# Two-layer hybrid encoder step: eleven weight places and three buffers of gathered rows in the expert stage

## What is computed

```python
def hier_moe(x, w_rg, b_rg, w_re, b_re, w_eg, w_eu, w_ed):   # 4 groups of 8 experts, hidden width 128
    g_w, g_idx = lax.top_k(pg, 1)                            # one group per row
    e_w, e_idx = lax.top_k(pe, EXP_TOPK)                     # two experts of that group
    ...
    for g in range(N_GROUPS):
        h = jax.nn.silu(jnp.einsum('nd,edf->nef', xf, w_eg[g])) * jnp.einsum('nd,edf->nef', xf, w_eu[g])
        out = out + jnp.einsum('nef,efd->nd', h * gate[:, g, :, None], w_ed[g])
    return out.reshape(b, t, d)

h = h + hier_moe(rms_norm(h, norm2), ...)
y = rms_norm(h, final_norm)                                  # after the last layer
```

## Time and profile before

| | us |
|---|---|
| runs: median (lowest to highest of 3) | 1532.16 (1531.15 to 1532.2) |
| profiled execution | 1534.14 |
| its span, first to last instruction | 1532.4 |
| TensorE busy in it | 1341.7 (88%) |
| VectorE, ScalarE, GpSimd busy | 527.1, 342.6, 220.3 |
| mean granted TensorE clock | 0.943 |
| DMA, mean over the span | 137 GB/s |

### The profile page before, as it was taken

One profiled execution on the slowest core, in us unless ns is written; L12 is line 12 of the kernel. 1 busy time (PEld: TensorE's weight loads), 2 busy tenths in 40 slices (PEclk: granted clock), 3 DMA queues, 4 the chain that ended last, 5 costly groups with the idle time before them and its releaser, 6 DMA issues. The chain is left out here.

```text
span 1532.4 us, 15151 instructions
## 1 busy us (share of the span) xinstructions
PE 1341.7 (88%) x5592; PEld 739.8 (48%) x5592; DVE 527.1 (34%) x1445; ACT 342.6 (22%) x773; POOL 220.3 (14%) x357
## 2 busy tenths in 40 slices
PE   6999899999999993987599999999999999569771
PEld 5654446544444452554385544564444445345440
DVE  1278884111011117221245789621100111442114
ACT  2142566100001010221213326531000010012112
POOL 5011051000000001232140200500000000023213
PEclk9999999999999995999799999999999999879986
DMA  8302102504105025899671220231060140649975
GB/s 227 110 12 56 56 1 68 165 0 137 70 0 206 0 78 195 311 411 402 252 192 59 56 63 1 63 103 68 0 205 0 45 161 0 233 157 410 408 293 216
DMA packets 94795, 210.32 MB, mean 137 GB/s; under 512 B 25392, under 2 KB 34832, under 8 KB 94720
## 3 DMA queue, kind: packets, MB, share of 16 engines
q1 hardware_dynamic: 81792, 183.90, 33.6%
q0 software_dynamic: 12928, 25.43, 4.8%
HBM read 196.29 MB, written 27.78 MB: 146 GB/s over the span
## 5 line engine op out<-in xcount | busy, mean ns | idle before, releaser
L689 PE MATMUL bank<-ring,xt 128*128 128x512 f32 (+1 forms) x1440 | 571.9, 553 | 2.8 <-issue 1.8
L689 PEld LDWEIGHTS bank<-ring,xt 128*128 128x128 f32 x1440 | 273.2, 192 | 272.6 <-issue 258.4
L1592 DVE TENSOR_TENSOR scr<-scr,bank 128x512 f32<-128x512 f32 x20 | 13.8, 688 | 368.6 <-PE bank L960 368.6
L507 POOL TENSOR_SCALAR stat<-stat 128x1 f32<-128x1 f32 (+1 forms) x27 | 10.3, 380 | 799.1 <-ACT uv L1106 617.2
L1250 ACT ACTIVATE scr<-bank,stat 128x512 f32<-128x512 f32 x40 | 25.3, 684 | 347.9 <-PE bank L689 347.8
L1026 PE MATMUL bank<-ring,xt 128*64 128x256 f32 x480 | 70.7, 402 | 17.1 <-issue 17.1
L720 PE MATMUL bank<-ring,xt 128*128 128x512 f32 x160 | 76.8, 614 | 0.0
L1026 PE MATMUL bank<-qkv,xt 128*64 128x256 f32 x256 | 70.2, 436 | 7.2 <-issue 7.2
L960 PE MATMUL bank<-ring,att 128*128 128x512 f32 x160 | 72.5, 596 | 2.2 <-ACT sgt L1242 1.8
L960 PE MATMUL bank<-ring,sgt 128*128 128x512 f32 x160 | 71.9, 592 | 0.0
L689 PE MATMUL bank<-more,xt 128*128 128x512 f32 x160 | 70.3, 592 | 0.0
(11 more groups left out here) (262 smaller groups left out, 1737.6 us busy)
## 6 DMA issues: line engine op xcount, KB each, us to landing
ring<-in_w_in SPq DMA_DIRECT2D x12, 2048.0 KB, 9.2
ring<-in_w_ed SPq DMA_DIRECT2D x36, 512.0 KB, 18.5
ring<-in_w_eg SPq DMA_DIRECT2D x30, 512.0 KB
ring<-in_w_eu SPq DMA_DIRECT2D x30, 512.0 KB
qkv<-in_w_eg SPq DMA_DIRECT2D x16, 512.0 KB
qkv<-in_w_eu SPq DMA_DIRECT2D x16, 512.0 KB
ring<-in_w_out SPq DMA_DIRECT2D x4, 2048.0 KB, 11.9
more<-in_w_ed SPq DMA_DIRECT2D x16, 512.0 KB, 12.6
```

What stands on the lines that cost most here:

```text
L689: mm = pe.matmul(out, xt[:, k, t * P:(t + 1) * P], rhs[:, k, :], start=(k == 0), stop=(k == KD - 1))
L1592: V.tensor_tensor(t1, t1, b[2][:, :], ALU.mult)
```

## The change

The expert stage gets an eleventh weight place and loses one of its four buffers of gathered rows; the space for the place comes from that buffer, from 24 more columns of `uv`, and from a part of `att`. Expert 10 is loaded ahead of the stage, just before the writes of x to `xd`. The loads in the stage go by pairs of units (11, 12), (13, 14) and so on, each after the block that used the place. The one-hots move from `att` to `uv`, the final norm's weights from `att` (loaded by GpSimd early in the last stage) to `qkv` (loaded by SP after block 16), the five targets of the squares become one with a wait between them, and the clearing of the gathered buffers' last columns moves behind the wait for the table.

```diff
-PLACES = 10
-XBUF = 4
+PLACES = 11
+XBUF = 3
-RING_FREE = 3 * PLACES // 2
+RING_FREE = 15
...
-        uv = sb("uv", [P, 2, NT, BLK])
+        uv_flat = sb("uv", [P, 2 * NT * BLK + 24])[:, :]
+        uv = uv_flat[:, 0:2 * NT * BLK].rearrange("p (c t w) -> p c t w", c=2, t=NT)
...
-        fin_gain = att_flat[:, 0:D]
-        onehot = att_flat[:, 0:2 * NT * (BR + UNITS)].rearrange("p (m c) -> p m c", m=2 * NT)
+        onehot = uv_flat[:, XW:XW + 2 * NT * (BR + UNITS)].rearrange("p (m c) -> p m c", m=2 * NT)
+        fin_gain = qkv_flat[:, 2048:2048 + D]
...
-                  (xt_flat[:, 2560:4608], ring_flat[:, 15360:16384])]
+                  (xt_flat[:, 2560:4608], ring_flat[:, 15360:16384]),
+                  (uv_flat[:, XW * XBUF:XW * XBUF + 2048], att_flat[:, 0:D])]
...
-        junk2 = [uv_flat[:, D * t:D * (t + 1)] for t in range(NT)]
+        junk2 = uv_flat[:, 0:D]
...
+                sp.wait_ge(mt_done, prior("mt_done", L) + 2 * NT)
+                expert(10, EXPERTS * L + 10)
                 for t in range(NT):
                     sp.wait_ge(xo_done, prior("xo_done", L) + 2 * t + 2)
                     sp.dma_start(xd[t * P:(t + 1) * P, 0:D], x[:, t, :]).then_inc(xd_out, 16)
...
-                def two_experts(b, rows):
-                    sp.wait_ge(gu_psum[L], b - PLACES // 2 + 1)
-                    for h in range(2):
-                        expert_up((2 * b + h) % PLACES, rows[h], up_in[(2 * b + h) % PLACES])
-                    sp.wait_ge(y_psum[L], b - PLACES // 2 + 1)
-                    for h in range(2):
-                        expert_down((2 * b + h) % PLACES, rows[h], down_in[(2 * b + h) % PLACES])
+                def units_in(units, rows):
+                    for e, row in zip(units, rows):
+                        sp.wait_ge(gu_psum[L], (e - PLACES) // 2 + 1)
+                        expert_up(e % PLACES, row, up_in[e % PLACES])
+                    for e, row in zip(units, rows):
+                        sp.wait_ge(y_psum[L], (e - PLACES) // 2 + 1)
+                        expert_down(e % PLACES, row, down_in[e % PLACES])
...
+                else:
+                    sp.wait_ge(y_psum[L], NB)
+                    sp.dma_start(fin_gain, a["final_norm"].partition_broadcast(P)).then_inc(s_gain, 16)
                 for z in range(YBUF):
...
                 for b in range(XBUF):
                     gather(b, b, x_in[b])
-                if L + 1 == DEPTH:
-                    pool.dma_start(fin_gain, a["final_norm"].partition_broadcast(P)).then_inc(s_rope, 16)
...
                     act.wait_ge(xo_done, prior("xo_done", L) + 2 * t + 2)
-                    squares(t, junk2[t], ss, sq_done)
+                    if t:
+                        act.wait_ge(sq_done, prior("sq_done", L) + t)
+                    squares(t, junk2, ss, sq_done)
...
                 dve.wait_ge(table_psum, prior("table_psum", L) + 1)
+                V.memset(xin_all[:, :, D:XW], 0.0)
...
                 then(ins)
-                V.memset(xin_all[:, :, D:XW], 0.0)
                 then(V.tensor_copy(w16[:, :, 0:NG], logit[:, :, 0:NG]))
...
-                    dve.wait_ge(s_rope, 32)
+                    dve.wait_ge(s_gain, 32 * DEPTH + 16)
```

More of the change, by code:

```diff
@@ L260, in build @@
         att_flat = att[:, :, :].rearrange("p a b -> p (a b)")
-        fin_gain = att_flat[:, 0:D]
-        onehot = att_flat[:, 0:2 * NT * (BR + UNITS)].rearrange("p (m c) -> p m c", m=2 * NT)
-        assert 2 * NT * (BR + UNITS) <= 1536
+        onehot = uv_flat[:, XW:XW + 2 * NT * (BR + UNITS)].rearrange("p (m c) -> p m c", m=2 * NT)
+        assert XW + 2 * NT * (BR + UNITS) <= XW * XBUF
         begun = counted[0:1, 0:n_over * EXPERTS].rearrange("p (b e) -> p b e", e=EXPERTS)
@@ L281, in build @@
                   in_ring[2], in_ring[3], in_ring[4],
-                  (xt_flat[:, 2560:4608], ring_flat[:, 15360:16384])]
+                  (xt_flat[:, 2560:4608], ring_flat[:, 15360:16384]),
+                  (uv_flat[:, XW * XBUF:XW * XBUF + 2048], att_flat[:, 0:D])]
         assert len(places) == PLACES
-        uv_flat = uv[:, :, :, :].rearrange("p c t w -> p (c t w)")
-        junk2 = [uv_flat[:, D * t:D * (t + 1)] for t in range(NT)]
+        junk2 = uv_flat[:, 0:D]
         xin_all = uv_flat[:, 0:XW * XBUF].rearrange("p (q c) -> p q c", q=XBUF)
@@ L460, in _ @@
                 expert(9, EXPERTS * L + 9)
-                def two_experts(b, rows):
-                    sp.wait_ge(gu_psum[L], b - PLACES // 2 + 1)
-                    for h in range(2):
-                        expert_up((2 * b + h) % PLACES, rows[h], up_in[(2 * b + h) % PLACES])
-                    sp.wait_ge(y_psum[L], b - PLACES // 2 + 1)
-                    for h in range(2):
-                        expert_down((2 * b + h) % PLACES, rows[h], down_in[(2 * b + h) % PLACES])
-                for b in range(PLACES // 2, PLAIN):
-                    two_experts(b, [EXPERTS * L + 2 * b, EXPERTS * L + 2 * b + 1])
+                def units_in(units, rows):
[5 more added lines that the diff above has]
+                        expert_down(e % PLACES, row, down_in[e % PLACES])
+                for e in range(PLACES, EXPERTS, 2):
+                    units = range(e, min(e + 2, EXPERTS))
+                    units_in(units, [EXPERTS * L + v for v in units])
                 sp.wait_ge(experts_known, prior("experts_known", L) + 1)
                 for v in range(0, ALWAYS, 2):
-                    two_experts(PLAIN + v // 2,
-                                [EXPERTS * L + sp.value_load(over_expert[:, v + h:v + h + 1], min_val=0, max_val=EXPERTS - 1)
+                    units_in(range(EXPERTS + v, EXPERTS + v + 2),
+                             [EXPERTS * L + sp.value_load(over_expert[:, v + h:v + h + 1], min_val=0, max_val=EXPERTS - 1)
                                  for h in range(2)])
```

## The result

| | us |
|---|---|
| before: median of the runs beside it | 1531.86 |
| after: median | 1593.45 (1591.56 to 1596.0) |
| ratio, with 95% interval | 1.0402 [1.0387, 1.0417] |
| span of the profiled execution, before and after | 1532.4, 1594.2 |

The change makes the kernel 61.6 us slower. The forecast was 1576.9 us within 1542 to 1595: the right side and the right mechanism, with 44.7 us of loss where 61.6 came.

The account below looks back on a forecast made before the run. TensorE, then weight arrival, bound the expert stages; the change would make a two-block loop bind. Seven 19.74 us pairs per layer add 26.9 and 24.7 us, last blocks give 5.9 and 1.0 back: 1532.2 + 44.7 = 1576.9 us, range 1542 to 1595.

Parts of the forecast that it names:

- The loop: Expert stage, three row buffers: two blocks take 4.29 us to the gather, L, then 6.70 us of work: 10.99 + L.
- D: In block timings, the end of a block's down products; as rival, a wash at L about 5.6: 1532 us, chance 0.04.
- the eleventh place's load: One expert loaded ahead per layer: covered by idle DMA, saving 3.84 us per layer only if weights set the end.
- L: Expert stage: time from a gather's start to the first transpose of its rows, taken as 7.9 us.
- rival A: Expert stage: gathers keep out of the weights' way and the eleventh place pays: 1524.5 us, chance 0.08.
- The clock term: Expert stage: lower granted clock after pauses slows TensorE; half of 1.69 us counted, 0.85 us per pair.
- The number of rounds: Expert stage: seven pairs of blocks per layer at 19.74 us each, up to the end of block 14.
- blocks 15 and 16: End of each expert stage: they gather nothing more and find their weights there, taking 9.0 us: -5.9 and -1.0 us.
- B: Expert stage: the clock falls in every block, pair 20.58 us: 1588.6 us; chance 0.08 for above 1592 to B and higher.
- C: Expert stage: the loop binds softly, L 6.5 us, no lower clock: 1545.3 us; chance with its neighbours 0.20.

Follow-up runs that it names:

- the runs with the small moves: The change with ten places and four buffers, so only the one-hots, norm weights, squares' target, pad columns and SP waits differ from the kernel before: 1531.77 us, ratio 0.9995.
- with four buffers: The change with eleven places but four buffers of gathered rows kept, the fourth in att: 1522.75 us, ratio 0.9939 to the kernel before.
- the run with small loads: The change with weight loads inside the expert stage bringing only 64 of 1024 columns each: 1524.39 us (one run).
- the turned queue: The change (eleven places, three buffers) with GpSimd issuing the next gather ahead of the scatter: 1523.05 us, ratio 0.9946 to the kernel before.
- the run with twelve filling matmuls: The change plus twelve matmuls with unused results ahead of the transposes of every second block from the fourth: 1632.37 us.

## Why the prediction was right, and where its sizes were off

**The loop** held step by step. From D to the gather 4.29 us were read; in eleven of the twelve rounds 4.27 to 4.31 came, in one 5.71. The transposes are released by the gather, though only in every second block, the up products no longer wait for weights, and without the buffer's loss nothing is lost (the runs with the small moves and with four buffers). Ahead of the stage the eleventh place's load stayed covered (DMA share 0.01 from 1372 to 1380; the first gather starts at 1379.80), and under the loop the place brought nothing, as the sum had it. Two of the prediction's signs came otherwise: pauses of 2 to 5 us in nearly each block, with D to D of 9 to 10.5, were expected, and the blocks came in twos, with 5.4 to 7.7 us ahead of every second one.

**L** was taken as 7.9 us. Over the twelve gathers that ended a long pause it was 8.10 to 9.83, mean 9.12. The step that failed was the reason for the low end: that bursts of weights would overlap less at the slower pace. The pace fell, but the blocks came in twos, 6.5 us apart, and so did SP's requests for their weights (from 1425.54 and from 1432.06 on); DMA stood at 1.00 to 1.03 from 1430 to 1445, through the whole gather and beyond. That the weights lengthen L is shown by the run with small loads. That it is the coming in twos which kept L at 9 is only argued; with the turned queue DMA was as full and L 7.66. For rival A the prediction drew on a page: "DMA: Bandwidth & Descriptors" of the Trainium skill (Queues, rings and completion order) has each DMA engine alternate between its queues by packets. The prediction's own reading of that, a gather only a packet or two behind, fails as a forecast: the gather came about 5 us later under load than with small loads (9.12 against 4.12), and the measurement decides. What the packets did no run shows, so the page's sentence is neither confirmed nor refuted here.

**The clock term** was as large a miss: 1.27 us a pair, where L's was 1.22. Pauses of 2.7 to 2.9 us in each block were assumed, at the border, and half of 1.69 us was counted. In fact one block of two has a pause of 5.4 to 7.7 us, always the one on the loop: its work, from the first transpose to the result copies, takes 8.1 to 9.5 us (mean 8.82 of twelve) where 6.70 stood, 2.12 more and not 0.85.

**The number of rounds** was off the other way. Seven pairs were counted, but the last gather, of block 16, meets hardly any weights (DMA share 0.14, in the stretch below), and its rows were there 3.32 us after its start at 1542.54: the last pair took 14.28 us in layer 1 and 13.20 in layer 0 in place of 19.74.

```profile
1542.50:1546.00 3.50, 2.31 (x15) 0.72 (x10) 0.35 (x1) 1.45 (x3) 1.11 (x2) 1.00 0.14 40
```

The balance: six pairs at 22.49 and 22.21 in place of 19.74 are 16.5 and 14.8 us more, the last pairs 5.5 and 6.5 less, 19.3 in all; 44.7 + 19.3 = 64.0, and 63.8 was measured in the two stages (blocks 15 and 16 took 8.94 and 8.93 us, for the 9.0 that were set). The 2.0 us outside the stages, which the prediction had not, are within what runs differ by.

That the time fell inside the range owes something to luck. The forecast time was 16.6 us too low; 1593.45 lies 1.5 us below the range's upper end and just above the band from 1562 to 1592 that had 0.60, in the part that had 0.08. L and the clock together were 31.3 us short over the twelve pairs, and the pairs counted too many hid 12.0 of them.

**The rivals.** A gave 1524.5 and its price was about right: with the rows in time, eleven places run at 1522.75 and 1523.05. It fell because L was never near its 5.6 in the rounds that count (8.10 at least). B's number, 1588.6, was nearest, but not its mechanism: the clock falls in every second block, not in each. C and D fell with L.

## What to carry to other kernels

A buffer in a loop is worth what stands between two uses of it: the issue queue ahead of the refill, the transfer as long as it is under load, and the work until the buffer is free again. Add these up and compare with the block times that the buffers left over cover; a prefetch whose rows come "just in time" in the trace has nothing to give. Before giving up a place elsewhere for such a buffer, or the reverse, look at what the refill queues behind: here, to issue the gather ahead of a scatter was worth 70 us of the changed kernel.

## What the runs showed of the hardware

Gathers overtake weights, but not unhindered. While a weight load took 20.54 us to land, gathers queued behind a scatter took about 9 us, beside a long backlog (8.85 in the earlier trace rows) as beside two blocks' loads (mean 9.12 in after). Queued ahead of the scatter, beside full weights, they took 7.66 us on average; behind it, beside small loads, 4.12.

No one length of pause tells whether the granted clock falls. In the kernel before, products after a pause of 1.19 us took 3.67 us and after 2.95 us 5.36; the prediction put the border near 2.85. In the run with twelve filling matmuls, block 3 of layer 1 kept its pace after 2.30 us (first row below). In the run with small loads 2.03 us were enough: transposes of 1.59 us in place of 1.16, and of two successive blocks (stretches, columns as above) one at a mean clock of 1.00, the other, with that pause, at 0.83:

```profile
1427.78 1.16 PE L1024 MATMUL bank<-ident,uv 128*128 128x128 f32 x8 [2.30 <-DMA uv<-xd,mb]
```

```profile
671.80:678.60 6.80, 6.59 (x49) 3.81 (x49) 1.64 (x3) 1.71 (x4) 2.44 (x4) 1.00 0.38 97
678.60:688.90 10.30, 8.35 (x50) 4.85 (x51) 1.64 (x3) 1.76 (x5) 2.43 (x4) 0.83 0.39 120
```
